# Rows copied to all partitions by float32r products of a high and a low part, in a block of attention and recurrence layers

## What is computed

```python
q = l2_normalize(q); k = l2_normalize(k)        # per token and head: x * rsqrt(sum(x*x) + eps)
g = -exp(a_log) * softplus(aa + dt_bias)        # per token and head
gc = cumsum(g in chunks); decay = exp(gc_i - gc_j)
o = chunk_gated_delta_rule(q, k, v, beta, g)
o = rms_norm(o, o_norm) * silu(z)               # per token and head
```

## Time and profile before

| | us |
|---|---|
| median of 3 runs | 1949.36 |
| lowest, highest | 1945.45, 1949.75 |
| profiled execution, its own time | 1946.41 |
| span of it, first to last instruction | 1944.6 |
| PE busy | 1930.8 (99%) |
| DVE busy | 1018.0 (52%) |
| ACT busy | 888.2 (46%) |
| POOL busy | 850.2 (44%) |

### The profile page before, as it was taken

One profiled execution on the slowest core, in us unless ns is written; L12 is line 12 of the kernel. 1 busy time (PEld: TensorE's weight loads), 2 busy tenths in 40 slices (PEclk: granted clock), 3 DMA queues, 4 the chain that ended last, 5 costly groups with the idle time before them and its releaser, 6 DMA issues.

```text
span 1944.6 us, 23731 instructions
## 1 busy us (share of the span) xinstructions
PE 1930.8 (99%) x9106; PEld 1532.8 (79%) x9106; DVE 1018.0 (52%) x1832; ACT 888.2 (46%) x1355; POOL 850.2 (44%) x644
## 2 busy tenths in 40 slices
PE   9999999999999999999999999999999999999999
PEld 6878887877788878787877888677766788888887
DVE  5757755555745668766464647575644436101210
ACT  6455553344345455543344355586555344312321
POOL 5545432433445454422434445455322445444443
PEclk9999999999999999999999999999999999999999
DMA  5334542423535235632414545322111332222232
GB/s 202 128 118 131 138 134 80 155 77 124 185 102 177 88 114 148 163 106 71 153 65 141 192 151 163 135 77 98 65 55 55 119 108 87 99 97 98 98 114 71
DMA packets 94575, 227.69 MB, mean 117 GB/s; under 512 B 29976, under 2 KB 33048, under 8 KB 93152
## 3 DMA queue, kind: packets, MB, share of 16 engines
q1 hardware_dynamic: 88768, 223.03, 35.1%
q10 hardware_dynamic: 5696, 3.15, 0.6%
HBM read 194.01 MB, written 24.64 MB: 112 GB/s over the span
## 4 chain that ended last, share of the span: by engine, by line
PE 86%; DVE 7%; DMA 2%; ACT 2%; SPq 1%; issue 1%; POOL 1%; ACTq 0%; DVEq 0%
PE bank L442 85%; DVE kv L376 1%; DVE ER L376 1%; PE bank L446 1%; SPq L371 1%; DMA X<-inverses 1%; DVE scs L401 1%; DMA kv<-blocks 1%; DVE tmp L376 1%; DVE m8s L398 0%; ACT lt L428 0%; DVE lt L386 0%; DVE tmp L386 0%; ACT wh L431 0%; DMA st<-units 0%
## 5 line engine op out<-in xcount | busy, mean ns | idle before, releaser
L376 POOL TENSOR_TENSOR wl<-st,wh 128x512 fp32r<-128x512 f32 x602 | 803.4, 1357 | 1020.2 <-ACT wh L431 1020.1
L442 PE MATMUL bank<-hh,wh 128*128 128x512 f32 x1616 | 651.2, 404 | 1.9 <-ACT hh L428 0.6
L442 PE MATMUL bank<-hh,wl 128*128 128x512 f32 x1616 | 629.2, 390 | 0.0
L442 PE MATMUL bank<-hl,wh 128*128 128x512 f32 x1616 | 628.8, 390 | 0.0
L431 ACT ACTIVATE wh<-st 128x1024 fp32r<-128x1024 f32 (+1 forms) x302 | 316.8, 1049 | 238.3 <-PE bank L442 190.5
L442 PEld LDWEIGHTS bank<-hh,wh 128*128 128x128 f32 x1616 | 303.3, 188 | 90.5 <-issue 26.0
L442 PEld LDWEIGHTS bank<-hl,wh 128*128 128x128 f32 x1616 | 303.6, 188 | 67.2 <-issue 6.9
L442 PEld LDWEIGHTS bank<-hh,wl 128*128 128x128 f32 x1616 | 303.3, 188 | 64.6
L376 DVE TENSOR_TENSOR xt<-xt,bank 128x512 f32<-128x512 f32 x40 | 27.4, 686 | 236.0 <-PE bank L442 236.0
L428 ACT ACTIVATE tmp<-bank 128x512 f32<-128x512 f32 x70 | 41.7, 596 | 158.2 <-PE bank L442 151.5
L442 PE MATMUL bank<-fh,wh 128*128 128x512 f32 x256 | 99.6, 389 | 0.0
(11 more groups left out here) (344 smaller groups left out, 2833.4 us busy)
## 6 DMA issues: line engine op xcount, KB each, us to landing
st<-units SPq DMA_DIRECT2D x300, 512.0 KB, 3.5
gates<-tmp SPq DMA_DIRECT2D x48, 256.0 KB, 2.7
gt<-gates SPq DMA_DIRECT2D x48, 256.0 KB, 3.6
pads<-tmp SPq DMA_DIRECT2D x32, 128.0 KB, 2.7
qk<-tmp SPq DMA_DIRECT2D x16, 256.0 KB, 4.2
x_scratch<-xt SPq DMA_DIRECT2D x2, 2048.0 KB, 8.7
xt<-x_scratch SPq DMA_DIRECT2D x2, 2048.0 KB, 8.2
ph<-phi SPq DMA_DIRECT2D x8, 512.0 KB, 4.7
```

The source lines that it names most:

```text
L376: return NOTHING if self.e is None else self.e.tensor_tensor(out, a, b, op)
L442: return NOTHING if self.e is None else self.e.matmul(out, lhsT, rhs, start=start, stop=stop, skip_group_check=share)
```

## The change

The three kinds of rows are made into one float32r tile each, in which some partitions hold the high part and others the low part of the value with the sign turned, and one float32r product with weights -1/16 or -1 adds them up.

- ACT copies each root tile to `mix` (rounded to float32r: `dn_hi`, `on_hi`), and DVE forms `mix = mix * later - root`: minus the high part (rounded on writing) in the first 16 partitions of a strip, high minus root, that is minus the low part, in the other 16. `spread` waits for this (`dn_mix`, `on_mix`), and its products have `spreadr[:, 0:1]` (-1/16) as weights.
- The weights of the small unit put the four columns of the decays at 32 to 35 and at 36 to 39, so all row operations on `R1` have 8 rows in place of 4. DVE adds a cast to `gx` and one more operation on it. The pair products read `gx` rows 32 to 39 for both heads, with columns of `spreadr[:, 1:5]`. SP's copy of `rw` to rows 96 to 99 goes.
- The constant `first` (128 columns) goes; `later`, `second` and `pick` (6 columns) come. A spacer tile holds the place, and `ctile` has one buffer less.

```diff
-    c.add("first", np.broadcast_to(i[:, None] % 32 == 0, (128, 128)))
+    c.add("later", i[:, None] % 32 >= 16)
+    c.add("second", (i[:, None] - 32) // 4 == 1)
+    c.add("pick", -1.0 * ((i[:, None] // 8 == 4) & (i[:, None] % 4 == np.arange(4))))
...
-    R0, R1, R2, R3 = slice(0, 4), slice(32, 36), slice(64, 68), slice(96, 100)
+    R0, R1 = slice(0, 4), slice(32, 40)
...
-        def spread(src, name, *key):
-
-            pe.wait_ge(*at(f"{name}_r", *key))
+        def spread(mix, name, *key):
+
+            pe.wait_ge(*at("spreadr"))
+            pe.wait_ge(*at(f"{name}_mix", *key))
             for c, q in enumerate(Q4):
-                t = pe.mm(bank(4 + c, f"{name}_row", *key, c), first[q, :], src[q, :], True, True)
+                t = pe.mm(bank(4 + c, f"{name}_row", *key, c), spreadr[q, 0:1].broadcast_to([32, 128]), mix[q, :], True, True)
...
                 if n in (0, 2):
-                    pe.wait_ge(*at("rows", l))
-                    for m, q in ((n, Q4[1]), (n + 1, Q4[3])):
-                        pe.mm(bank(4 + m % 2, "G", l, m), ident[q, q.start + m:q.start + m + 1].broadcast_to([32, 128]), L.rw[q, :], True, True).then_inc(*sig("h_g", l, m))
+                    pe.wait_ge(*at("pick"))
+                    pe.wait_ge(*at("g_mix", l))
+                    for m in (n, n + 1):
+                        pe.mm(bank(4 + m % 2, "G", l, m), spreadr[R1, 1 + m:2 + m].broadcast_to([8, 128]), L.gx[R1, :], True, True).then_inc(*sig("h_g", l, m))
...
                 rnorm(aa4[f][:], banks[4 + f][:], 4 + f, ("dn", l, f), "dn_r", l, f)
+                ac.wait_ge(*at("dn_r", l, f))
+                ac.cp(L.mix[f][:], aa4[f][:]).then_inc(*sig("dn_hi", l, f))
...
                     rnorm(L.aa4[0][:], banks[4][:], 4, ("on", l), "on_r", l, scale=1.0 / 128.0)
+                    ac.wait_ge(*at("on_r", l))
+                    ac.cp(L.mix[0][:], L.aa4[0][:]).then_inc(*sig("on_hi", l))
...
+        def mixed(mix, x, name, *key):
+
+            dv.wait_ge(*at(f"{name}_hi", *key))
+            dv.stt(mix[:], mix[:].bitcast(F32), C("later"), x[:], ALU.mult, ALU.subtract).then_inc(*sig(f"{name}_mix", *key))
...
                 if f == 0:
+                    for m in range(2):
+                        mixed(L.mix[m], aa4[m], "dn", l, m)
                     yield
...
+                    dv.wait_ge(*at("small_v", l, 4))
+                    dv.cp(L.gx[R1, :], L.rw[R1, :]).then_inc(*sig("g_hi", l))
+                    dv.wait_ge(*at("g_hi", l))
+                    dv.stt(L.gx[R1, :], L.gx[R1, :].bitcast(F32), C("second")[R1, :], L.rw[R1, :], ALU.mult, ALU.subtract).then_inc(*sig("g_mix", l))
...
         def front3(l):
             L = layer[l]
-            yield from idle(3)
+            yield from idle(2)
+            mixed(L.mix[0], L.aa4[0], "on", l)
+            yield
             dv.wait_ge(*at("on_up", l))
...
-            yield from idle(7)
-            sp.wait_ge(*at("small_v", l, 4))
-            sp.dma(L.rw[R3, :], L.rw[R1, :]).then_inc(*dma("rows", l))
-            yield from idle(3)
+            yield from idle(10)
```

More of the change, by code:

```diff
@@ L103, in pack_units @@
             w = I["w_in"][key[1]]
-            for c0, at, m in ((2048, 0, 4), (5448, 4, 4), (2052, 32, 4), (5384, 64, 64)):
+            for c0, at, m in ((2048, 0, 4), (5448, 4, 4), (2052, 32, 4), (2052, 36, 4), (5384, 64, 64)):
                 u[:, :, at:at + m] = kmajor(w[:, c0:c0 + m]).reshape(128, 8, m)
@@ L248, in pack_columns @@
         put(f"conv{l}", I["conv_w"][l].reshape(4, 12, 128).transpose(2, 1, 0).reshape(128, 48))
-        c[32:36, at[f"alog{l}"][0]] = I["a_log"][l]
-        c[32:36, at[f"dt{l}"][0]] = I["dt_bias"][l]
+        c[32:40, at[f"alog{l}"][0]] = np.tile(I["a_log"][l], 2)
+        c[32:40, at[f"dt{l}"][0]] = np.tile(I["dt_bias"][l], 2)
         put(f"onorm{l}", I["dn_onorm"][l][:, None])
@@ L291 @@
     "act_small": "small_a lam_a",
-    "act_heads": "dn_sq dn_r on_sq on_r egl gexp h_eg h_dt h_vb h_xt",
+    "act_heads": "dn_hi on_hi dn_sq dn_r on_sq on_r egl gexp h_eg h_dt h_vb h_xt",
     "act_rows": "pl_p qk_sq qk_r q2_sq q2_r k2_sq k2_r conv_0 conv2_0 conv_th zc_a pl_a ga_a gelu_a rec_a",
@@ L296 @@
     "pool_zero": "vcz0 sC0",
-    "dve_small": "colx identr rw0 hb2 small_v hn gcol lam kz0 gs",
-    "dve_heads": "h_e h_n h_k vn0 sc_e inv",
+    "dve_small": "spreadr colx identr pick rw0 hb2 small_v hn gcol lam kz0 gs",
+    "dve_heads": "dn_mix on_mix g_hi g_mix h_e h_n h_k vn0 sc_e inv",
     "dve_rows": "qi ki qk_n qk_o q2_n q2r k2_n k2r rope conv_v conv2 gelu rec_v",
@@ L531, in build @@
     identr = sb("identr", [128, 128], F32R)
+    spreadr = sb("spreadr", [128, 5], F32R)
+    sb("gaps", [128, 120])
     col = sb("col", [128, cols.shape[1]])
@@ L594, in build @@
         L.cdiag = sb(f"cdiag{l}", [128, 128], stack=dtmp)
+        L.mix = [sb(f"mix{f}{l}", [128, T], F32R, stack=dtmp) for f in range(2)]
+        L.gx = sb(f"gx{l}", [128, T], F32R, stack=dtmp)
         dtmp.close()
@@ L658, in build @@
     hid = sb("hid", [128, 2, 128], stack=comp)
-    ctile = [sb(f"ctile{i}", [128, 32], stack=comp) for i in range(4)]
+    ctile = [sb(f"ctile{i}", [128, 32], stack=comp) for i in range(3)]
     comp.close()
@@ L702, in build @@
     ident, ones, mean, blk, eps = C("ident"), C("ones"), C("mean"), C("blk"), C("eps")
-    first = C("first")
     lc = colx[:, 8:48]
@@ L922, in delta @@
             yield
-            spread(aa4[0], "dn", l, 0)
+            spread(L.mix[0], "dn", l, 0)
             yield
-            spread(aa4[1], "dn", l, 1)
+            spread(L.mix[1], "dn", l, 1)
             yield
@@ L1051, in front3 @@
                 if j == 2:
-                    spread(L.aa4[0], "on", l)
+                    spread(L.mix[0], "on", l)
                 yield
@@ L2681, in vector_program @@
         dv.set(pad[1][:], 0.0).then_inc(*sig("warm"))
+        dv.wait_ge(*at("warm"))
+        dv.ts(spreadr[:, 0:1], pad[1][:, 0:1], -1.0 / 16.0, ALU.add).then_inc(*sig("spreadr"))
         dv.wait_ge(*at("norm_col"))
@@ L2691, in vector_program @@
         dv.cp(identr[:], ident).then_inc(*sig("identr"))
+        dv.cp(spreadr[:, 1:5], C("pick")).then_inc(*sig("pick"))
         for l in range(2):
```

## The result

| | before | changed |
|---|---|---|
| median, us | 1948.97 (4 runs) | 1969.31 (4 runs) |
| lowest, highest | 1945.45, 1949.75 | 1968.42, 1970.22 |
| profiled execution, its own time | 1946.41 | 1970.22 |
| span of it | 1944.6 | 1968.3 |
| mean granted clock | 1.000 | 0.994 |

The changed kernel is slower: the ratio is 1.0108, with a 95% interval of 1.009 to 1.0125. The medians alone lie 20.3 us apart, a ratio of 1.0104. On the profiled executions it is 23.8 us, where the sum had 23.2. The two differ because the profiled execution of before is near its lowest time and that of the changed kernel is its highest. The median was forecast at 1971.0, within 1963 to 1978.

The account below looks back on a forecast made before the run. PE was taken to bound the kernel (busy 1930.8 of 1944.6 us). Terms -5.5 + 1.6 + 22.9 + 4.2 = +23.2 us gave 1969.6 from the profiled 1946.41; allowing for the higher median, forecast 1971, range 1963 to 1978.

Parts of the forecast that it names:

- The spreads: Six row spreads on PE, heads and output norm: float32r gains 0.63 us each, 3.8 us in all.
- The decays: Four pairs G on PE: two steps in place of four, 0.43 us less a pair, 1.7 us in all.
- The stop at the heads' first spread: PE waits 0.8 us in each layer for DVE's mix, behind the index queries; cost 1.6 us.
- The stop at the output norm: PE waits 11.45 us in each layer for DVE's mix, behind the last selection and its mask; cost 22.9 us.
- The clock: After each long output norm stop PE restarts at half pace, costing 2.1 us, twice: 4.2 us.
- rival (a): The stalls come but the clock stays at 2.4 GHz: +19.0 us, 1965.4 on the profiled run; chance 0.15.
- Rival (c): The clock takes longer to come back, up to 8.4 us in all: +27.4, 1974 to 1976; chance 0.12.
- Rival (d): Output norm's mix is ready when PE comes, taken between selection rounds: 1942.5 (1945.4 from the median); chance 0.03.
- Rival (e): The products stay in float32, so the gain is missing but the stalls come: +28.7, 1975; chance 0.02.
- delayed by 1.4 us: DVE after the heads' first mix: second mix and two gx operations delay it 1.4 us, covered by 1.77 us idle.

Follow-up runs that it names:

- filler: The changed kernel with 46 float32r products, their results overwritten, ahead of each output norm spread, so PE is busy while it waits; 1965.5 us, ratio 1.0099.
- on_early: The changed kernel with DVE's output norm mix issued after the sixth of sixteen rounds of the last selection, not behind its mask; 1943.65 us, ratio 0.9986.
- one_strip: on_early with all four products of every spread reading strip 0, so every head gets head 0's root; 1947.14 us, ratio 1.0004.
- both_early: on_early with the heads' first mix also moved on DVE, ahead of the index queries; 1943.63 us, ratio 0.9981.
- on_k10: on_early with the output norm's mix issued behind the eleventh of sixteen selection rounds, not the sixth; 1955.35 us, ratio 1.0046.

## Why the prediction was right

The sum had +23.2 us on the profiled execution, and it was +23.8. Term by term:

- **The spreads, 0.63 us each:** 0.63, from the table; 0.44 us to the next product where 0.4 was forecast. The reading that a float32 spread is one float32 product and 0.40 us of change between full array and strips held, and the 0.40 stays in float32r.
- **The decays, 0.43 us a pair:** 0.40, from 1.06 to 0.66. Both products' loads stand within 0.29 us, the second while the first product runs on the same rows:

```profile
140.84 0.29 PEld L444 LDWEIGHTS bank<-gx,spreadr 8*128 8x128 f32 x2 [0.35 <-issue]
```

  A bare second load of 0.19 us on top of the 0.65 forecast would have made 0.84. The rule of the Trainium skill (TensorE: Matmul & The Clock Gate, Part 3, Packing small matmuls), that a load overlaps only when its row group differs, is not borne out here.
- **The stop at the heads' first spread, 0.8 us:** 0.76, with 0.44 us for the products behind it. Against before it costs 0.2 us net.
- **The stop at the output norm, 11.45 us:** 11.27 and 11.26 in the waits. The mask took 0.43 us once POOL was idle (forecast 0.47), the mix 0.74 (0.69).
- **The clock, 2.1 us each:** 1.9 and 2.1. The mechanism was right, but so close a figure was luck: it was read from the start of the program, and the same price was 1.5 to 3.0 us a stop in the other kernels, and 2.3 and 1.7 in the two layers of one. The Trainium skill (TensorE: Matmul & The Clock Gate, The HAM clock gate) has the slow state as the default, and the trace agrees: the granted clock went to 0.50 in a PE without work. So rival (a) falls; filler is what it described. Rival (c), a clock that comes back more slowly, falls too. Rival (d) is what on_early is: had the mix been ready, the kernel would have been faster, as that rival had it (1942.5 on the profiled execution; on_early's was 1943.04). Rival (e) falls with the rows of the spread, which have four records and 0.44 us where float32 had eight and 1.07.
- **What was not in the sum:** with the two profiled executions laid side by side, PE's stream gains 0.9 us in the first 23 us and 0.8 at 539, and loses 1.8 us at the products on `X` in layer 1, behind the DMA of the inverses. The three nearly cancel, which is luck as well. The start differs by about as much among kernels that share it, and the wait for the inverses lay between 0.4 and 3.3 us a layer in the ten profiles, the change made or not, so I take them for differences between executions; that was argued, not tested. A part of the longer wait could be the change's own, since PE comes sooner to `X` when its products ahead are shorter. Some steps of 0.3 us elsewhere make up the rest.

One statement was mis-sized, although it cost nothing. DVE was to be delayed by 1.4 us after the heads' mixes. Its timeline shows more:

```profile
118.10 1.41 DVE L388 SCALAR_TENSOR_TENSOR mix<-mix,cst,ER 128x512 fp32r<-128x512 f32 x2
...
122.01 1.83 DVE L388 SCALAR_TENSOR_TENSOR Y<-Y 8x512 f32<-8x512 f32 x1
...
124.46 2.19 DVE L397 TENSOR_TENSOR_SCAN rw<-cst,Y 8x512 f32<-8x512 f32 x1
126.69 1.33 DVE L391 CAST gx<-rw 8x512 fp32r<-8x512 f32 x1
128.06 0.74 DVE L388 SCALAR_TENSOR_TENSOR gx<-gx,cst,rw 8x512 fp32r<-8x512 f32 x1
128.83 0.69 DVE L378 TENSOR_TENSOR qi<-tmp,tabs 128x512 f32<-128x512 f32 x1
```

The operation at 128.83 stood at 125.25 before, so DVE is 3.6 us later there, though PE's stream is 1.3 us earlier. The scan takes 2.19 us where it took 1.21, and the operation on `Y` 1.83 where it took 0.69: shifted by the mixes, they now fall beside POOL's operations of 120.76 to 123.30 and from 124.14 on. That they have 8 rows now in place of 4 is not the reason: with 8 rows the one on `Y` took 0.68 in on_early and the scan 1.21 in one_strip. The operation at 128.83 took 1.60 us before and 0.69 now, out of POOL's way, and the next one likewise, so that DVE is only 1.6 us later when it comes to `kf`. The forecast had counted each operation at its time in the trace of before. PE asks for none of this until 140.85, so it stayed hidden; both_early, which moves the same operations again, found a wait.

## What to carry to other kernels

An operation that is put into an in-order queue inherits all that stands ahead of it. Before a product waits for a new producer, read in that producer's order how late it already runs: here DVE was over 10 us behind PE at this place, and harmless as long as PE only wrote for it and didn't read from it. When PE is the bound, a short operation that it will need belongs between two steps of a long side task, ahead of the time at which PE comes to it; moved so, the same change is a gain of 0.14%. And in this kernel each stop of PE of 3.2 to 11.3 us on the output norm cost its own length and about 2 us more for the clock, so a stop of 3 us is not a cheap one.

## What the runs showed of the hardware that was not expected

- After a stop of 3.2 us (on_k10, layer 1) the products behind it still ran at 1.2 GHz, for some 6 us of PE's work, and this was the dearest of the clock's costs (3.0 us). With 11.3 us of stop it was 4 us of work and 2.0. The length of the stop did not set the price.
- Side by side with POOL's work, some of DVE's operations took over twice as long: the mix of 128 x 512 took 1.84 us in place of 0.74, and the one of 8 x 512 on `Y` 1.83 in place of 0.68. Others didn't: the rounds' MAX8 and MATCH_REPLACE8 kept their 0.69 and 0.68 beside POOL's operations from 350.21 on, and in the kernel before, DVE's four operations on `qf` and the banks took 2.48 us beside POOL's operation of 120.30 to 122.86, and the four on `kf` 2.47 with none beside them. So such a DVE operation has no one duration, and one moved by a microsecond can change its own. That POOL's work is the cause is read from the times side by side; no run took it away.
